# Order of the two matmuls in every 512-column product, and the order of the first loads, in a four-layer transformer kernel

## The reference

```python
# first block, layer l (0: attention and gating, 1: retention)
h = rmsnorm(x, norm_mix[l]);  x = x + mixer(h)
h = rmsnorm(x, norm_ffn[l]);  x = x + (silu(h @ w_gate[l]) * (h @ w_up[l])) @ w_down[l]     # 1024 -> 2816 -> 1024
# second block, layer l
x = layer_norm(alpha * x + 0.5 * swiglu_2(x, w_ff1_in[l], w_ff1_out[l]), ...)               # 1024 -> 4096 -> 1024
x = layer_norm(alpha * x + hybrid_mixer(x, ...), ...)
x = layer_norm(alpha * x + 0.5 * swiglu_2(x, w_ff2_in[l], w_ff2_out[l]), ...)
```

## Time and profile before

| | |
|---|---|
| median of three runs | 2287.16 us |
| the profiled execution: time | 2286.68 us |
| the profiled execution: span of its instructions | 2284.9 us |
| TensorE (PE) busy | 2271.5 us, 99% |
| TensorE weight loads (PEld) busy | 2058.5 us, 90% |
| VectorE (DVE) busy | 1783.0 us, 78% |
| ScalarE (ACT) busy | 1286.1 us, 56% |
| DMA, mean | 181 GB/s |
| mean granted TensorE clock | 0.999 of full |

### The profile page before, as it was taken

One profiled execution on the slowest core, in us unless ns is written; L12 is line 12 of the kernel. 1 busy time (PEld: TensorE's weight loads), 2 busy tenths in 40 slices (PEclk: granted clock), 3 DMA queues, 4 the chain that ended last, 5 costly groups with the idle time before them and its releaser, 6 DMA issues.

```text
span 2284.9 us, 37627 instructions
## 1 busy us (share of the span) xinstructions
PE 2271.5 (99%) x15111; PEld 2058.5 (90%) x15111; DVE 1783.0 (78%) x2713; ACT 1286.1 (56%) x2016; POOL 79.6 (3%) x96
## 2 busy tenths in 40 slices
PE   9999999999999999999999999999999999999998
PEld 8988889998888888999999888988889999998887
DVE  7898658879758876897679886698767976798854
ACT  7855455655445544585666554465545856565542
POOL 0022000002100000020000000000000200000000
PEclk9999999999999999999999999999999999999999
DMA  6466565446556566554455555566665543556563
GB/s 242 138 196 191 189 209 175 150 157 220 176 183 212 191 189 193 200 176 130 132 174 193 192 192 188 165 201 203 189 191 200 175 138 121 183 181 217 187 184 100
DMA packets 115084, 412.45 MB, mean 181 GB/s; under 512 B 12896, under 2 KB 14304, under 8 KB 114656
## 3 DMA queue, kind: packets, MB, share of 16 engines
q1 hardware_dynamic: 114336, 406.91, 55.6%
q0 software_dynamic: 288, 2.10, 0.3%
q10 hardware_dynamic: 288, 1.05, 0.1%
HBM read 408.96 MB, written 1.05 MB: 179 GB/s over the span
## 4 chain that ended last, share of the span: by engine, by line
PE 88%; DVE 8%; ACT 2%; issue 1%; DMA 0%; SPq 0%; POOL 0%; DVEq 0%; ACTq 0%
PE ps L452 87%; DVE wlo L2012 3%; DVE region L2804 1%; ACT whi L1250 1%; ACT region L1472 1%; DMA raw<-in_ew_c 0%; PE ps L721 0%; DVE region L2331 0%; DVE RX L2201 0%; DVE x L2059 0%; DVE region L2334 0%; DVE x L2208 0%; DVE region L2447 0%; DVE region L2474 0%; DVE region L2973 0%
## 5 line engine op out<-in xcount | busy, mean ns | idle before, releaser
L452 PE MATMUL ps<-xx,whi 128*128 128x512 f32 (+1 forms) x4504 | 1202.9, 353 | 3.7 <-DVE xx L2067 2.4
L2012 DVE TENSOR_TENSOR wlo<-raw,whi 128x1024 fp32r<-128x1024 f32 (+3 forms) x772 | 925.5, 1207 | 273.3 <-ACT whi L1250 272.2
L1250 ACT ACTIVATE whi<-raw 128x1024 fp32r<-128x1024 f32 (+3 forms) x772 | 801.1, 1043 | 517.5 <-PE ps L452 506.8
L452 PEld LDWEIGHTS ps<-xx,wlo 128*128 128x128 f32 x3696 | 694.2, 188 | 118.7 <-DVE wlo L2012 0.2
L452 PE MATMUL ps<-xx,wlo 128*128 128x256 f32 x3696 | 796.8, 279 | 0.0
L452 PEld LDWEIGHTS ps<-xx,whi 128*128 128x128 f32 x4504 | 690.8, 188 | 9.1 <-issue 3.2
L452 PE MATMUL ps<-H,whi 128*128 128x512 f32 (+1 forms) x2144 | 539.0, 339 | 0.1
L452 PE MATMUL ps<-H,wlo 128*128 128x256 f32 x1632 | 364.0, 279 | 0.0
L452 PEld LDWEIGHTS ps<-H,wlo 128*128 128x128 f32 x1632 | 306.4, 188 | 46.8
L452 PEld LDWEIGHTS ps<-H,whi 128*128 128x128 f32 x2144 | 329.6, 188 | 1.6 <-issue 0.6
L2007 DVE TENSOR_REDUCE t<-ps 128x256 f32<-128x512 f32 x320 | 219.7, 688 | 41.1 <-PE ps L452 37.0
(11 more groups left out here) (316 smaller groups left out, 1592.5 us busy)
## 6 DMA issues: line engine op xcount, KB each, us to landing
raw<-in_sg SPq DMA_DIRECT2D x128, 512.0 KB, 4.2
raw<-in_su SPq DMA_DIRECT2D x128, 512.0 KB, 4.2
raw<-in_sd SPq DMA_DIRECT2D x128, 512.0 KB, 4.1
raw<-in_mw_g SPq DMA_DIRECT2D x48, 512.0 KB, 3.7
raw<-in_fg SPq DMA_DIRECT2D x44, 512.0 KB, 3.3
raw<-in_fu SPq DMA_DIRECT2D x44, 512.0 KB, 3.3
raw<-in_fd SPq DMA_DIRECT2D x32, 512.0 KB, 3.5
raw<-in_mw_a SPq DMA_DIRECT2D x24, 512.0 KB, 4.1
```

What stands on the lines that cost most here:

```text
L452: return e.matmul(out, lhsT, rhs, start=start, stop=stop, skip_group_check=True)
L1250: e.activation(m.whi[:, c % NHL, 0:cw], m.raw[:, c % NRAW, 0:cw], ACT.Copy).then_inc(s["whi"].h, s["whi"].up(c))
L2012: e.tensor_tensor(m.wlo[:, c % NHL, 0:cw], m.raw[:, c % NRAW, 0:cw], m.whi[:, c % NHL, 0:cw].bitcast(F32), ALU.subtract).then_inc(s["wlo"] ...
```

## The change

`mm2` loses its flag and always issues hi, then lo. The buffers stay where they are. At the front, `WARM` goes from 14 to 18; ScalarE's queue now issues `pk` in place of the two halves of x; SyncE's queue issues the two halves of x behind the first weight chunk, where it issued `pk`.

```diff
-WARM = 14
+WARM = 18
...
-    turn = [0]
-
     def mm2(b, wh, wl, a, start):
 
-        turn[0] ^= 1
-        if turn[0]:
-            mm(b[:, :], wh, a.rearrange("p a b -> p (a b)"), start=start, stop=False)
-            return mm(b[:, 0:256], wl, a[:, 0, :], start=False, stop=True)
-        mm(b[:, 0:256], wl, a[:, 0, :], start=start, stop=False)
-        return mm(b[:, :], wh, a.rearrange("p a b -> p (a b)"), start=False, stop=True)
+        mm(b[:, :], wh, a.rearrange("p a b -> p (a b)"), start=start, stop=False)
+        return mm(b[:, 0:256], wl, a[:, 0, :], start=False, stop=True)
...
-    for p in range(2):
-        e.dma_start(m.x[:, 4 * p:4 * p + 4, :], ins["x"][:, 4 * p:4 * p + 4, :]).then_inc(
-            s[f"x{p}"].h, s[f"x{p}"].up("in", by=16))
+    e.dma_start(m.pk[:, :], ins["pack"]).then_inc(s["pk"].h, s["pk"].up("in", by=16))
...
         if c == 1:
-            load("pk", "in", m.pk[:, :], ins["pack"])
+            for p in range(2):
+                load(f"x{p}", "in", m.x[:, 4 * p:4 * p + 4, :], ins["x"][:, 4 * p:4 * p + 4, :])
```

## The result

The changed kernel takes 2315.16 us (median of four runs, 2309.25 to 2318.78) against 2287.11 us; the ratio is 1.012 with a 95% interval of 1.0106 to 1.0135. It is slower by about 28 us, in the direction forecast and 3 us from the forecast of 2312. Its runs scatter over 9.5 us, those of the kernel before over 0.3 us. The profiled execution took 2316.28 us with a span of 2314.5 us, 29.6 us more than the span before.

A forecast was written before the change was run, and what follows sets the result against it. The prediction took TensorE, busy for 99% of the span, as the bound. From the profiled 2286.7 us, +26.7 us for the order and -0.7 us for the front gave 2312.7, stated as 2312 us; range 2284 to 2322 us.

The forecast's parts named there:

- The bound: Whole program: TensorE, busy for 99% of the span, sets the time; a slower TensorE stream is paid in full.
- the indifferent case: Rival, wide products: order of hi and lo doesn't matter, only the front counts; 2286 us, no measurable change; chance 0.12.
- The order term: Wide products: alternating hi and lo costs 351.7 ns per pair, 6.7 ns more, times 4000 pairs: +26.7 us.
- the slow pace: TensorE's slower pace for 256-column matmuls, 117.8 ns each; a hi and a lo would take 353 ns.
- The step from rows 8: Start of a wide run: two adjacent hi seem to lift the stream out of 353 ns; the new order has none.
- The front term: Program start: first real matmul 0 to 1.1 us earlier, perhaps at full clock; -0.7 us, bounds -1.6 to +0.5.
- The fast pace for the new order: Rival, wide products: the hi lo stream keeps 340 ns per pair; -20 us, 2266 us; chance 0.10.
- The pace between: Wide products: pairs settle halfway at 346.5 to 349 ns; +6 to +16 us, 2292 to 2302 us; chance 0.18.
- The rule of the Trainium skill: Wide products: matmul distance is N/2.4 + 2.5 ns whatever stands beside; 325 ns per pair in either order, order term zero.

The follow-up runs named there:

- group2: Kernel before with wide products issued as two hi, then two lo, except the first four chunks of a feed-forward stage; 2284.36 us, ratio 0.9988.
- group4: Kernel before with wide products issued as four hi, then four lo in a bank; 2288.03 us, ratio 1.0005.
- group8: Kernel before with wide products issued as eight hi, then eight lo in a bank; 2282.79 us, ratio 0.9982.
- lo_first: Wide products as hi lo at a bank's first tile, then lo hi at all others, against the kernel before; 2307.24 us, ratio 1.0089.
- front_only: Kernel before with only the new front and 18 products of ones, old wide order; 2286.80 us, ratio 0.9999.
- order_only: Kernel before with only the new order of the wide product (`mm2` as in the change), front as before; 2316.61 us, ratio 1.0125.
- wplace64_new: New order, front as before, with whi, wlo and x 64 bytes further on, against the kernel before; 2310.48 us, ratio 1.0103.
- shift128: Kernel before with xx, H and buffers between them at 128 instead of 64 in their 512-byte lines; new order 2312.44 us, old order 2301.13 us.
- shift192: Kernel before with xx, H and buffers between them at 192 instead of 64 in their 512-byte lines; new order 2314.40 us, old order 2287.82 us.
- psum_half: New order, but lo added into the second half of the bank (columns 256 to 511), against the kernel before; 2311.87 us, ratio 1.0107.
- shift128_new: New order, front as before, with xx, H and buffers between them at 128 instead of 64, against the kernel before; 2312.44 us.

## Why the prediction was right, and where it was off

*The bound.* Right: TensorE's stream, paid in full. +29.9 us in the wide pairs against +29.6 us in the span. The whole range, 2284 to 2322 us, took in the indifferent case as well, so that the time lies in it says little; the forecast's own 2305 to 2320 held too.

*The order term.* It was sized at +6.7 ns per pair and +26.7 us, and measured +7.5 ns and +29.9 us. The two rows that it averaged, 350 ns of ew_pe and 353.3 ns of the slow pace, turned out to be near the two kinds of long stretch that occur: 349 and 353 ns. That their average, 351.7 ns, came within 1.3 ns of the 353.0 measured is in part luck: nothing in the prediction said how many stretches get which, and most of the profiled execution got the slower. Eight pairs at the faster one take 2.79 us, under the 2.81 to 2.83 that were to be seen everywhere. The step from rows 8 held in its result: orders in which equal widths stand side by side (group2, group4, group8) keep 345 to 346 ns, and with the buffers where they were every alternating one is slower. It was too simple in three things. The two hi do not lift the stream out of a pace that it then keeps; in lo_first the pairs are back at 349 to 353 ns soon behind each meeting. Not only hi but lo too is cheaper beside its like (116.0 against 120.2 ns). And the alternation has two paces of its own, which the places of the buffers change; its 353 ns are not the three 117.8 ns of the narrow products that I had made them out of (hi 233.2 and lo 120.2, not 235.6 and 117.8).

*The front term.* Sized at -0.7 us; front_only measured no difference (0.9999), and 0.05 us are left at the sums of the squares. The start at 8.17 us and the full clock came as I had listed them, the first chunk even 0.99 us earlier where I had allowed 0.8, but ScalarE then waited 0.69 us for x. The step that failed is that an earlier end of the first chunk's products is an earlier end of what follows. With them over at 11.5 us, the second chunk's wlo was late, because ScalarE and VectorE come to it only behind the tiles of x, and then the fourth chunk, which lands when it did before. One row was miscounted: from 8.99 to 12.15 there are 14 matmuls and not 15, so 225 ns each and not 211; the 1.4 us would be 1.5. All this is below what a measurement can tell.

*The rivals.* The indifferent order fell with order_only. The fast pace for the new order fell too: no long stretch of any new-order kernel is under 346 ns. (Moving the weight buffers brought 347 ns, wplace64_new.) The pace between came true in part, as the 349 ns stretches; the best of the four runs, 2309.25 us, is still above the 2302 us that I gave that case. The rule of the Trainium skill that the distance of two matmuls is N/2.4 + 2.5 ns ("TensorE: Matmul & The Clock Gate", "Back-to-back issue gap") would have left the time unchanged; measured pairs are 6 to 9% above its 325 ns and depend on order and place. The prediction left out that the section gives this formula for a matmul that stands alone, and says that in a stream with weight loads the spacing is set by both; the rule was a weaker rival than it was made to look.

*What stays open.* What in the hardware makes the paces. That it is an interplay of reading moving tiles and reading weight tiles fits shift128, shift192 and wplace64_new, and psum_half doesn't contradict it, but it is not shown: the buffers that were moved are also written and read by ScalarE and VectorE, and no run kept those apart. What gives a stretch one of its paces is open too.

## What to carry to other kernels

When TensorE is the bound and full, measure its pace from starts over many matmuls, not from durations, and compare it between stretches of the same shapes: a difference of a few ns per matmul is a per cent of the program. In this kernel matmuls of equal width did better side by side than long and short ones in turn, in three layouts, by 0.5 to 1.3%; try that, and try the places of the operands within their lines together with the order. An earlier start at the front is worth nothing if a later wait, here the one that goes back to the fourth chunk, ends when it did before.

## What the runs showed of the hardware that I had not expected

- A stream of matmuls of the same shapes has more than one steady pace at the same granted clock: 113.3 or 117.8 ns for 256 columns, 349 or 353 ns for a pair of 512 and 256. A stretch keeps its own, over 1000 pairs in the longest.
- Which pace a stretch gets can differ between two executions with the same program text there (862 matmuls in 150 us in order_only against 851 in the changed kernel), and the runs of the changed kernel scatter by 9.5 us, where those of the kernel before scatter by 0.3. The order alone doesn't make the scatter: shift128_new and wplace64_new, in the new order too, scatter by 0.2 us.
- Moving the moving tiles by 64 bytes cost the kernel with the old order 14 us (2301.13 against 2287.05 us); by 128 bytes nothing in sum (2287.82), with the wide pairs slower by 6.4 us and the narrow products faster by 6.5.
- The clock of the first chunk stayed at its 2.4 GHz level when TensorE's idle time ahead of it fell from 2.43 to 1.30 us; it had been at the 1.2 GHz level for 3.3 us before.
